# One order of width classes, one form of down product: a mixture-of-experts layer on Trainium2

## The chip, the cores and the metric

The kernel runs on one core of a Trainium2 chip. TensorE (PE) multiplies, with its weight loads shown apart (PEld); VectorE (DVE), ScalarE (ACT) and GpSimd (POOL) work beside it; SyncE (SP) issues the large transfers. The metric is the device time of one launch in microseconds (us), the median over runs. Every trace below is one profiled execution.

## The reference, cut to what matters

A decoder layer over 1024 tokens of 1024 channels: a recurrent branch and an attention branch (their code is untouched), then a mixture of experts. A router picks 4 of 32 experts for every token. For each expert, with its own weights:

```
gu  = x_blk @ w_gate_up[e] + b_gate_up[e]        # 1024 -> 2048
g   = min(gu[:, :1024], 7);  u = clip(gu[:, 1024:], -7, 7)
act = (u + 1) * (g * sigmoid(1.702 * g))
y   = act @ w_down[e] + b_down[e]                # 1024 -> 1024
out[token] += gate * y                           # on top of the residual
```

The 4096 pairs of token and expert are spread unevenly. The reference's routing of its own inputs gives these tokens per expert, sorted: 56, 69, 72, 85, 92, 100, 107, 108, 111, 112, 117, 119, 119, 122, 124, 128, 131, 132, 138, 141, 143, 145, 148, 155, 157, 158, 160, 162, 167, 168, 172, 178. No expert has over 256, so there are 32 items of work, one for each expert.

## The kernel before, in words

Stages A to C compute the two branches and the router. Stage D counts the tokens of each expert on DVE (L1420 to L1503), gives each item a width class from `WIDTHS` (L34) and sorts the items by class, widest first. Stage E works through them. `by_class` (L1657) writes one loop for each class on every engine, with the matmuls cut to `w` columns; items of one class follow one another.

One item `i` of width `w`, by engines:

- SP loads 12.6 MB of weights through six slots of 2 MB (`load`, L1700), each as soon as DVE has consumed it; two orders of the loads, for items up to `n_wide` and behind it (L1742).
- The weights come as 12 chunks: c0 to c7 gate and up, c8 to c11 down. A chunk is split into two half-precision parts: ACT makes the high part (`split_hi`, L1861), DVE the rest (`split_lo`, L1975, with `largest` for a later check). Rings of six (four in narrow items) hold the parts.
- PE makes three half-precision passes over a split chunk (`split_chunk`, L2181). An item with `w >= 128` (`halves`, L1642) does this for all 12 chunks. A narrower item does it for c0 to c7 and multiplies the down chunks in float32 straight from the staged weights (`whole_chunk`, L2196).
- DVE clips gate and up (L2035, L2042) and makes the product (L2052); where down is split too, ACT rounds it (L1920) and DVE takes the rest (`activated_lo`, L2057, signal `a_s`). DVE's order is fixed: clip of chunk c, then split of chunk c+4.
- At an item's end PE turns the next item's gathered rows (`turn_rows`, L2137) in groups of four transposes: two groups of 128 tokens when `w` is at most 128, four otherwise. ACT (L1869) and DVE (L2004) split what came out, cut to the columns that the present width needs; the order by falling width makes that enough for the next item. The third and fourth group come after PE's wait for the last `a_s` (L2239).
- ACT then alternates `y_bias` (L1912, out of PSUM), the next item's `split_hi` for c0 to c3, and the gated rows `y_part` (L1880); it reloads a table (L1929) and splits c4 of the new item. POOL gathers rows (L1783) and adds the results to the output (L1797).

The order of PE around an item's end (L2234 to L2243):

```
down_lo_sy(0); pe.wait_ge(a_s, NP * i + 3)
down(0, 0, 6); down_lo_sy(1); down(1, 0, 6)
pe.wait_ge(a_s, NP * i + 4)
down(0, 6, KT)
for g in range(2, 2 * blocks(w)): turn_rows(i + 1, g, w, ...)
down(1, 6, KT)
for j in range(2, NP): down_lo_sy(j); down(j); turn_y(i, j - 2, w)
```

and of ACT (L1948 to L1967): x_part 0 and 1, next_hi(0), x_part 2 and up, y_bias(0), next_hi(1), y_bias(1), next_hi(2), y_bias(2), y_part(0), next_hi(3), y_bias(3), y_part(1).

Of the kernel before, what the change touches and what calls it, by code (L numbers as in the profile page):

```python
# [21 lines left out]
P = 128  # L22
# [1293 lines left out]
def stage_d(nc, m, a):  # L1316
# [9 lines left out]
    with ExitStack() as ctx:  # L1326
# [87 lines left out]
        def _(dve):  # L1414
# [13 lines left out]
            step(dve.tensor_tensor(kind[:], over[:, 1:NV + 1, :], over[:, 0:NV, :], ALU.subtract))  # L1428
# [62 lines left out]
            for g in range(0, NG, BATCH):  # L1491
# [60 lines left out]
def stage_e(nc, m, a, fast):  # L1552
# [21 lines left out]
    with ExitStack() as ctx:  # L1574
# [82 lines left out]
        def by_class(eng, n_items, early, body):  # L1657
# [12 lines left out]
            with eng.If(early[-1] > 0):  # L1670
                lo = 0
                for v in range(EARLY):
                    one_class(lo, early[v], WIDTHS[v])
                    lo = early[v]
                eng.nop()
            lo = early[-1]
            for v in range(EARLY, NV):
                hi = border(eng, v)
                one_class(lo, hi, WIDTHS[v])
                lo = hi  # L1680
# [18 lines left out]
        def _(sp):  # L1699
# [10 lines left out]
            def run():  # L1710
# [31 lines left out]
                if fast:  # L1742
                    n_wide = sp.value_load(m.n_wide[0:1, 0:1], min_val=0, max_val=ITEMS - 1)
                    with sp.If(n_wide > 0):
                        with sp.Fori(0, n_wide) as i:
                            e_next = expert(sp, i + 1)
                            load_up(i, e_next)
                            load_down(i, e_next)
                            load_later(i)
                        sp.nop()  # L1750
                    with sp.If(n_items - 1 > n_wide):
                        with sp.Fori(n_wide, n_items - 1) as i:
                            e_next = expert(sp, i + 1)
# [106 lines left out]
        def _(act):  # L1860
# [3 lines left out]
            def x_part(i, g, w, first=False):  # L1864

                act.wait_ge(x_mm, NP * i + x_step(w) * (g + 1))
                k0, b = 4 * (g % 2), g // 2
                n = min(w - b * P, P)
                act.activation((x_hi if fast else x_f)[:, k0:k0 + 4, b * P:b * P + n],  # L1869
                               x_bank(g, first)[:].rearrange("p a (b n) -> p (a b) n", n=P)[:, :, 0:n], ACT.Copy, scale=SX  # L1870
                               ).then_inc(x_hi_s, x_step(w))
# [14 lines left out]
            def run():  # L1886
# [3 lines left out]
                for g in range(NP):  # L1890
                    x_part(0, g, CHUNK, True)
# [7 lines left out]
                def body(i, w):  # L1899
# [5 lines left out]
                    def y_bias(j):  # L1905
# [3 lines left out]
                        if fast and not halves(w) and j % 2 == 1:  # L1909
                            act.sem_inc(down_lo_s, 2)  # L1910
                        for h in range(2):
                            ins = act.activation(y_t[:, 2 * j + h, 0:w], p_d[j % 2][:, h, 0:w], ACT.Identity,  # L1912
                                                 bias=bias[:, 16 + 2 * j + h:17 + 2 * j + h],
                                                 scale=1.0 / SW / SA if halves(w) else 1.0 / S2)
# [15 lines left out]
                    for c in range(NG):  # L1930
                        if c % 2 == 1:
                            silu(c // 2)
                        if halves(w):
# [3 lines left out]
                            split_hi(c + RI, ring(c + RI, w))  # L1937
                            if c % 2 == 1:
                                activated_hi(c // 2)
                        else:  # L1940
                            act.wait_ge(gu_mm, NG * i + c + 1)
                            if fast:
                                cc = c + RI
                                act.wait_ge(w_in[slot(cc % NG)], 16 * (i + cc // NG + 1))
                                split_hi(cc % NG, ring(cc, w))
# [14 lines left out]
                    if halves(w):  # L1960
                        next_hi(2)
                    y_bias(2)
                    y_part(i, 0, blocks(w))
                    if halves(w):
# [9 lines left out]
        def _(dve):  # L1974
# [15 lines left out]
            def fold(k, wide):  # L1990
# [3 lines left out]
                dve.wait_ge(down_peak_s, NP * (k + 1) if wide else NP)  # L1994
# [3 lines left out]
            def x_part(i, g, w, first=False):  # L1998
                dve.wait_ge(x_hi_s, NP * i + x_step(w) * (g + 1))
                b = g // 2  # L2000
                n = min(w - b * P, P)
                k0 = 4 * (g % 2)
                r = (slice(None), slice(k0, k0 + 4), slice(b * P, b * P + n))
                dve.scalar_tensor_tensor(out=x_lo[r], in0=x_bank(g, first)[:].rearrange("p a (b n) -> p (a b) n", n=P)[:, :, 0:n],  # L2004
                                         scalar=SX, in1=x_hi[r], op0=ALU.mult, op1=ALU.subtract).then_inc(x_lo_s, x_step(w))
# [4 lines left out]
            def run():  # L2010
                if fast:
# [5 lines left out]
                    for g in range(NP):  # L2017
                        x_part(0, g, CHUNK, True)
# [3 lines left out]
                def body(i, w):  # L2022
# [24 lines left out]
                    def product(j):  # L2047
# [4 lines left out]
                        dve.scalar_tensor_tensor(out=up[j % 2][:, :, 0:w] if halves(w) else a_f[:, 2 * j:2 * j + 2, 0:w],  # L2052
# [319 lines left out]
```

## Time and profile before

| what | value |
|---|---|
| median of 3 runs | 1895.47 us (1894.23 to 1898.2) |
| span of the profiled execution | 1890.9 us, so 4.6 us under the median |
| PE busy | 1792.1 us (95%) |
| DVE busy | 1427.3 us (75%) |
| ACT busy | 1252.4 us (66%) |
| POOL busy | 429.0 us (23%) |
| mean granted clock | 0.978 |
| moved | 479.08 MB |

The span runs from the first to the last instruction. The profiled execution's own time is this span and what lies around it; the 4.6 us are taken for the latter. Stage E begins at 591.5 us. The forms of its matmuls tell the classes: one item each of 184 and 176 columns, three of 168, four of 160, two of 152, three of 144, two of 136, six of 128, five of 112 and five of 96.

### The profile page before, as it was taken

The page shows a single profiled execution, that of the slowest core. Times are in us where ns is not written, and L with a number is a line of the kernel's source. Part 1 is how long each engine was busy: PE and PEld are TensorE (multiplying, and loading weights), DVE is VectorE, ACT ScalarE, POOL GpSimd, SP SyncE. Part 2 cuts the span into 40 slices and gives each one's busy share as a digit, 9 for nine tenths or more (in the row PEclk, how much of TensorE's full clock was granted, in tenths as well). Part 3 has the DMA queues.
Part 4 walks back from the last instruction along what each step waited for, and adds up shares of the span by engine and source line. Part 5 has one row for each costly group of instructions (what it writes and reads, how often), then busy time and mean ns, then how long its engine had stood idle before and what let it go on. Part 6 is the DMA issues. An engine that isn't in the chain of part 4 may idle for free.

```text
span 1890.9 us, 54214 instructions
## 1 busy us (share of the span) xinstructions
PE 1792.1 (95%) x21982; PEld 1645.4 (87%) x21982; DVE 1427.3 (75%) x2714; ACT 1252.4 (66%) x1661; POOL 429.0 (23%) x304
## 2 busy tenths in 40 slices
PE   8999988988987999999999999999999999999996
PEld 7777765667866999999999999998999899999996
DVE  5553647765357888888888889999999977767755
ACT  6565337873114777777777888778887876657654
POOL 4000000001003111111112322323233334434433
PEclk9999999999987999999999999999999999999998
DMA  5211001004539889999999999999999999999993
GB/s 152 56 45 45 23 28 41 1 1 151 175 120 346 287 297 306 307 308 328 321 323 321 335 327 345 324 349 341 352 366 351 359 357 372 373 375 375 367 374 111
DMA packets 251409, 479.08 MB, mean 253 GB/s; under 512 B 17312, under 2 KB 38096, under 8 KB 251264
## 3 DMA queue, kind: packets, MB, share of 16 engines
q1 hardware_dynamic: 231040, 443.59, 64.8%
q0 software_dynamic: 20256, 33.94, 8.2%
q8 instruction: 77, 1.26, 0.3%
q14 instruction: 36, 0.29, 0.0%
HBM read 466.96 MB, written 47.19 MB: 272 GB/s over the span
## 4 chain that ended last, share of the span: by engine, by line
PE 40%; DVE 11%; issue 11%; ACT 6%; DVEq 0%; ACTq 0%; POOLq 0%; POOL 0%
PE E_p_d L2200 6%; DVE E_w_lo L1984 6%; PE E_p_g L2188 4%; PE E_p_g L2190 4%; PE E_p_g L2191 4%; PE E_p_u L2190 4%; PE E_p_u L2188 4%; PE E_p_u L2191 4%; PE E_p_d L2188 3%; PE E_p_d L2191 3%; PE E_p_d L2190 3%; ACT E_w_hi L1862 3%; DVE E_up L2042 2%; PE E_p_t L2146 2%; PE E_p_t L2161 2%
## 5 line engine op out<-in xcount | busy, mean ns | idle before, releaser
L1984 DVE SCALAR_TENSOR_TENSOR E_w_lo<-E_w_st,E_w_hi 128x2048 f16<-128x2048 f32 x348 | 794.8, 2284 | 28.8 <-ACT E_w_hi L1862 27.4
L1862 ACT ACTIVATE E_w_hi<-E_w_st 128x2048 f16<-128x2048 f32 x348 | 661.4, 1906 | 25.4 <-PEq L1326 24.2
L2188 PE MATMUL E_p_g<-E_x_hi,E_w_hi 128*128 128x128 f16 (+9 forms) x2048 | 368.7, 223 | 4.2 <-DVE E_w_lo L1984 4.0
L2190 PE MATMUL E_p_g<-E_x_lo,E_w_hi 128*128 128x128 f16 (+9 forms) x2048 | 368.6, 223 | 1.5 <-issue 1.5
L2188 PE MATMUL E_p_u<-E_x_hi,E_w_hi 128*128 128x128 f16 (+9 forms) x2048 | 366.9, 222 | 2.1 <-DVE E_w_lo L1984 2.1
L2191 PE MATMUL E_p_g<-E_x_hi,E_w_lo 128*128 128x128 f16 (+9 forms) x2048 | 368.6, 223 | 0.0
L2190 PE MATMUL E_p_u<-E_x_lo,E_w_hi 128*128 128x128 f16 (+9 forms) x2048 | 366.8, 222 | 0.0
L2191 PE MATMUL E_p_u<-E_x_hi,E_w_lo 128*128 128x128 f16 (+9 forms) x2048 | 366.8, 222 | 0.0
L2188 PE MATMUL E_p_d<-E_a_hi,E_w_hi 128*128 128x128 f16 (+7 forms) x1408 | 280.1, 230 | 21.8 <-DVE E_a_lo L2059 17.9
L2190 PE MATMUL E_p_d<-E_a_lo,E_w_hi 128*128 128x128 f16 (+7 forms) x1408 | 280.1, 230 | 0.0
L2191 PE MATMUL E_p_d<-E_a_hi,E_w_lo 128*128 128x128 f16 (+7 forms) x1408 | 280.0, 230 | 0.0
L1797 POOL DMA_INDIRECT out<-E_y_rows,E_idx_out x66 | 153.0, 2317 | 485.1 <-ACT E_y_rows L1880 464.1
L2188 PEld LDWEIGHTS E_p_g<-E_x_hi,E_w_hi 128*128 128x128 f16 x2048 | 201.1, 98 | 6.1 <-DVE E_w_lo L1984 4.9
L2188 PEld LDWEIGHTS E_p_u<-E_x_hi,E_w_hi 128*128 128x128 f16 x2048 | 200.4, 98 | 2.8 <-DVE E_w_lo L1984 2.8
L2191 PEld LDWEIGHTS E_p_g<-E_x_hi,E_w_lo 128*128 128x128 f16 x2048 | 201.1, 98 | 1.8 <-issue 1.7
L2190 PEld LDWEIGHTS E_p_g<-E_x_lo,E_w_hi 128*128 128x128 f16 x2048 | 201.1, 98 | 0.7
L2190 PEld LDWEIGHTS E_p_u<-E_x_lo,E_w_hi 128*128 128x128 f16 x2048 | 200.4, 98 | 0.4
L2191 PEld LDWEIGHTS E_p_u<-E_x_hi,E_w_lo 128*128 128x128 f16 x2048 | 200.4, 98 | 0.0
L2188 PEld LDWEIGHTS E_p_d<-E_a_hi,E_w_hi 128*128 128x128 f16 x1408 | 139.0, 99 | 27.7 <-DVE E_a_lo L2059 17.8
L2200 PE MATMUL E_p_d<-E_a_f,E_w_st 128*128 128x112 f32 (+1 forms) x1280 | 150.2, 276 | 6.5 <-DVE E_a_f L2052 6.4
L2200 PEld LDWEIGHTS E_p_d<-E_a_f,E_w_st 128*128 128x128 f32 x1280 | 146.0, 192 | 10.1 <-issue 6.1
L2190 PEld LDWEIGHTS E_p_d<-E_a_lo,E_w_hi 128*128 128x128 f16 x1408 | 139.1, 99 | 0.7
(408 smaller groups left out, 3293.3 us busy)
## 6 DMA issues: line engine op xcount, KB each, us to landing
E_w_st<-in_w_gate_up SPq DMA_DIRECT2D x130, 2048.0 KB, 10.8
E_w_st<-in_w_down SPq DMA_DIRECT2D x64, 2048.0 KB, 10.8
A_w_st<-in_w_in SPq DMA_DIRECT2D x20, 512.0 KB, 3.9
A_x_rows<-in_x SPq DMA_DIRECT2D x8, 512.0 KB, 8.0
C_x_res<-in_x SPq DMA_DIRECT2D x8, 512.0 KB, 4.6
x_rows<-C_x SPq DMA_DIRECT2D x8, 512.0 KB, 5.1
out<-C_x SPq DMA_DIRECT2D x8, 512.0 KB, 5.9
h_rows<-C_h SPq DMA_DIRECT2D x8, 512.0 KB, 4.4
```

Of the source, the lines that this page charges most:

```text
L1797: pool.indirect_dma_start(a.out[0], bass.IndirectOffsetOnAxis(ap=idx_out[:, b:b + 1], axis=0), y_rows[:, b, :], None, bounds_check=token_m ...
L1862: act.activation(w_hi[r][:], staged(c), ACT.Copy, scale=SW).then_inc(hi_s if c < NG else down_hi_s, 1)
L1984: dve.scalar_tensor_tensor(out=w_lo[r][:], in0=staged(c), scalar=SW, in1=w_hi[r][:], op0=ALU.mult, op1=ALU.subtract, accum_out=total[:, c: ...
L2042: ins = dve.tensor_scalar(up[j % 2][:, h, 0:w], p_u[j % 2][:, h, 0:w], bias[:, 8 + 2 * j + h:9 + 2 * j + h], S1 * (LIMIT + 1.0), ALU.add, ...
L2146: ins = pe.transpose(bank[:, q // 2, (q % 2) * P:(q % 2 + 1) * P], rows[:, g // 2, k * P:(k + 1) * P], m.ident[:])
L2161: ins = pe.transpose(p_t[j % 2][:, b, h * P:(h + 1) * P], y_t[:, 2 * j + h, b * P:(b + 1) * P], m.ident[:])
L2188: pe.matmul(o_, wh, hi[:, k, 0:w], start=h == 0 and k == 0, stop=False, skip_group_check=True)
L2190: pe.matmul(o_, wh, lo[:, k, 0:w], start=False, stop=False, skip_group_check=True)
L2191: ins = pe.matmul(o_, wl, hi[:, k, 0:w], start=False, stop=k == KT - 1, skip_group_check=True)
L2200: ins = pe.matmul(banks[:, h, 0:w], staged(c)[:, k, h * P:(h + 1) * P], x[:, k, 0:w], start=h == 0 and k == 0, stop=k == KT - 1, skip_grou ...
```

## The change

The class list gets finer at its narrow end (120, 104, 88 and 72 are new) and the items are ordered so that a class of the wide half and one of the narrow half follow each other: 256, 192, then 184, 128, 176, 120, 168, 112, 160, 104, 152, 96, 144, 88, 136, 72. With the counts above the order of items is 184, 3 x 128, 176, 3 x 120, 3 x 168, 4 x 112, 4 x 160, 104, 2 x 152, 96, 3 x 144, 88, 2 x 136, 3 x 72. Every item splits all 12 chunks and makes its down products in three half-precision passes; the float32 form is left to the fallback. Every item turns all four groups of the next item's rows, 128 columns each, since the next item may be wider. SP has one order of loads. `n_wide` and its instruction go; stage D's class difference is written in two instructions.

```
-WIDTHS = (256, 192, 184, 176, 168, 160, 152, 144, 136, 128, 112, 96)
+WIDTHS = (256, 192, 184, 176, 168, 160, 152, 144, 136, 128, 120, 112, 104, 96, 88, 72)
-HALVES = 128
+FIRST = 2
+PAIRS = (NV - FIRST) // 2
+ORDER = WIDTHS[:FIRST] + tuple(WIDTHS[FIRST + PAIRS * side + v] for v in range(PAIRS) for side in range(2))
...
-            step(dve.tensor_tensor(kind[:], over[:, 1:NV + 1, :], over[:, 0:NV, :], ALU.subtract))
+            step(dve.tensor_tensor(kind[:, 0:FIRST, :], over[:, 1:FIRST + 1, :], over[:, 0:FIRST, :], ALU.subtract))
+            step(dve.tensor_tensor(kind[:, FIRST:NV, :].rearrange("p (v a) e -> p a v e", a=2), ...
...
-        def halves(w):
-            return fast and w >= HALVES
-        def ring(c, w):
-            return c % RING if halves(w) else c % RI
+        def ring(c):
+            return c % RING
...
-                    one_class(lo, early[v], WIDTHS[v])
+                    one_class(lo, early[v], ORDER[v])
...
-                    n_wide = sp.value_load(m.n_wide[0:1, 0:1], min_val=0, max_val=ITEMS - 1)
...
+                    with sp.Fori(0, n_items - 1) as i:
+                        e_next = expert(sp, i + 1)
+                        load_up(i, e_next)
+                        load_down(i, e_next)
+                        load_later(i)
...
-                n = min(w - b * P, P)
-                act.activation((x_hi if fast else x_f)[:, k0:k0 + 4, b * P:b * P + n],
+                act.activation((x_hi if fast else x_f)[:, k0:k0 + 4, b * P:(b + 1) * P],
...
-                    for g in range(2, 2 * blocks(w)):
-                        x_part(i + 1, g, w)
+                    for g in range(2, 2 * NB):
+                        x_part(i + 1, g)
                     y_bias(0)
-                    if halves(w):
+                    if fast:
                         act.wait_ge(gu_mm, NG * i + NG)
                         next_hi(1)
...
-                    if halves(w):
-                        x_part(i + 1, 0, w)
-                        x_part(i + 1, 1, w)
+                        x_part(i + 1, 0)
+                        x_part(i + 1, 1)
                         split_lo(NG * (i + 1) + 1, 0, 0, True)
-                        for g in range(2, 2 * blocks(w)):
-                            x_part(i + 1, g, w)
+                        for g in range(2, 2 * NB):
+                            x_part(i + 1, g)
                         for c in range(1, RI):
                             split_lo(NG * (i + 1) + c + 1, c, c, True)
...
                     def down(j, k0=0, k1=KT):
-                        if halves(w):
+                        if fast:
                             split_chunk(NG + j, p_d[j % 2], a_hi, a_lo, k0, k1)
...
-                    for g in range(2, 2 * blocks(w)):
-                        turn_rows(i + 1, g, w, lambda: pe.wait_ge(x_out_s, NP * (i + 1) + g - 1))
+                    for g in range(2, 2 * NB):
+                        turn_rows(i + 1, g, lambda: pe.wait_ge(x_out_s, NP * (i + 1) + g - 1))
```

## Rows read from the trace of the kernel before

**Rows 1.** The page, parts 1 and 2: busy time; GB/s in 40 slices.

```profile
PE 1792.1 (95%) x21982; PEld 1645.4 (87%) x21982; DVE 1427.3 (75%) x2714; ACT 1252.4 (66%) x1661; POOL 429.0 (23%) x304
GB/s 152 56 45 45 23 28 41 1 1 151 175 120 346 287 297 306 307 308 328 321 323 321 335 327 345 324 349 341 352 366 351 359 357 372 373 375 375 367 374 111
```

**Rows 2.** Windows over stage E: items of 184 to 136; 128 to 96; the last.

```profile
core 0: us, PE busy (x) PEld busy (x) DVE busy (x) ACT busy (x) POOL busy (x), PEclk, DMA share, GB/s
591.50:1292.00 700.50, 692.38 (x9729) 685.05 (x9729) 615.39 (x1108) 534.86 (x671) 167.41 (x114) 0.99 0.94 322
1292.00:1840.10 548.10, 525.32 (x8365) 518.12 (x8365) 449.85 (x863) 395.48 (x498) 200.31 (x105) 0.99 1.03 364
1840.10:1890.90 50.80, 34.93 (x544) 33.85 (x541) 28.42 (x66) 23.40 (x33) 17.46 (x9) 0.89 0.40 130
```

**Rows 3.** Windows of one item each: 168, 160, 136, 128, 128, 112, 96 columns.

```profile
739.10:784.70 45.60, 45.40 (x610) 45.17 (x608) 39.06 (x70) 33.77 (x43) 8.79 (x7) 1.00 0.90 305
917.70:961.40 43.70, 43.50 (x610) 43.26 (x609) 38.39 (x70) 33.58 (x43) 8.45 (x7) 1.00 0.92 316
1210.40:1250.30 39.90, 38.35 (x610) 37.59 (x610) 37.16 (x69) 32.43 (x43) 12.28 (x7) 1.00 0.99 344
1329.10:1366.90 37.80, 34.83 (x599) 34.27 (x597) 36.48 (x68) 31.61 (x39) 12.46 (x7) 1.00 1.01 359
1404.70:1443.90 39.20, 36.37 (x598) 35.70 (x597) 37.52 (x70) 32.62 (x39) 12.45 (x7) 0.96 1.01 358
1591.60:1627.50 35.90, 35.86 (x535) 35.54 (x534) 25.66 (x51) 23.12 (x30) 14.07 (x7) 1.00 1.05 374
1734.60:1769.80 35.20, 33.63 (x535) 33.01 (x533) 25.12 (x51) 22.47 (x30) 14.26 (x7) 1.00 1.04 373
```

**Rows 4.** Waits within the 160-column item: who waited, for whom, us, times, longest.

```profile
DVE E_gate L2035 <- PE E_p_g L2191: 1.3, 1, 1.3
PE E_p_d L2188 <- ACT E_y_t L1912: 0.2, 1, 0.2
```

**Rows 5.** Timeline of DVE, end of a 128-column item (start, us, engine, line).

```profile
1358.90 0.42 DVE L2059 SCALAR_TENSOR_TENSOR E_a_lo<-E_up,E_a_hi 128x256 f16<-128x256 f32 x1
1359.68 1.29 DVE L2004 SCALAR_TENSOR_TENSOR E_x_lo<-E_p_t,E_x_hi 128x512 f16<-128x512 f32 x2 [0.20 <-DVE E_peak_min L1996]
1371.97 2.29 DVE L1984 SCALAR_TENSOR_TENSOR E_w_lo<-E_w_st,E_w_hi 128x2048 f16<-128x2048 f32 x1 [0.84 <-ACT E_w_hi L1862]
```

**Rows 6.** Timeline of ACT, end of the same item.

```profile
1360.32 0.63 ACT L1912 ACTIVATE E_y_t<-E_p_d,E_bias 128x128 f32<-128x128 f32 x2 [0.40 <-PE E_p_d L2191]
```

**Rows 7.** Timeline of DVE, end of a 136-column item.

```profile
1240.07 0.43 DVE L2059 SCALAR_TENSOR_TENSOR E_a_lo<-E_up,E_a_hi 128x272 f16<-128x272 f32 x1
```

**Rows 8.** Timeline of ACT, end of the same 136-column item.

```profile
1242.84 0.20 ACT L1869 ACTIVATE E_x_hi<-E_p_t 128x32 f16<-128x32 f32 x1 [0.40 <-PE E_p_t L2146]
1242.93 0.63 ACT L1912 ACTIVATE E_y_t<-E_p_d,E_bias 128x136 f32<-128x136 f32 x2
```

**Rows 9.** Groups by line and form: count, busy us, mean ns, idle before.

```profile
L1869 ACT ACTIVATE E_x_hi<-E_p_t 128x512 f16<-128x512 f32 x44 | 23.5, 584 | 0.0
L2004 DVE SCALAR_TENSOR_TENSOR E_x_lo<-E_p_t,E_x_hi 128x512 f16<-128x512 f32 x44 | 28.4, 686 | 3.3 <-DVE E_peak_min L1996 1.2
L2035 DVE TENSOR_SCALAR E_gate<-E_p_g,E_bias 128x128 f32<-128x128 f32 x48 | 14.5, 344 | 1.8 <-PE E_p_g L2191 1.3
L2035 DVE TENSOR_SCALAR E_gate<-E_p_g,E_bias 128x112 f32<-128x112 f32 x40 | 11.3, 325 | 5.4 <-PE E_p_g L2191 5.2
L1912 ACT ACTIVATE E_y_t<-E_p_d,E_bias 128x128 f32<-128x128 f32 x48 | 15.2, 377 | 3.2 <-PE E_p_d L2191 3.0
L1912 ACT ACTIVATE E_y_t<-E_p_d,E_bias 128x112 f32<-128x112 f32 x40 | 12.0, 351 | 38.4 <-PE E_p_d L2200 38.4
```

**Rows 10.** Window inside the second 128-column item of Rows 3.

```profile
1436.30:1439.70 3.40, 3.32 (x34) 3.09 (x32) 3.40 (x6) 3.40 (x6) 0.00 (x0) 0.50 1.05 382
```

**Rows 11.** Timeline of DVE in stage D: first and last of nine class instructions.

```profile
551.57 0.59 DVE L1426 TENSOR_TENSOR D_over<-D_rem,limit 128x416 f32<-128x416 f32 x1
557.73 0.80 DVE L1445 TENSOR_REDUCE D_jump<-D_start 128x32 f32<-128x384 f32 x1
```

More of the change, by code:

```diff
@@ L1427, in _ @@
                                    m.limit[:].unsqueeze(2).to_broadcast([P, NV + 1, E_]), ALU.is_gt))
-            step(dve.tensor_tensor(kind[:], over[:, 1:NV + 1, :], over[:, 0:NV, :], ALU.subtract))
+            step(dve.tensor_tensor(kind[:, 0:FIRST, :], over[:, 1:FIRST + 1, :], over[:, 0:FIRST, :], ALU.subtract))
+            step(dve.tensor_tensor(kind[:, FIRST:NV, :].rearrange("p (v a) e -> p a v e", a=2),
+                                   over[:, FIRST + 1:NV + 1, :].rearrange("p (a v) e -> p a v e", a=2),
+                                   over[:, FIRST:NV, :].rearrange("p (a v) e -> p a v e", a=2), ALU.subtract))
             step(dve.tensor_copy(share[:], kind[:]))
@@ L1862, in split_hi, with x_part @@
                 act.activation(w_hi[r][:], staged(c), ACT.Copy, scale=SW).then_inc(hi_s if c < NG else down_hi_s, 1)
-            def x_part(i, g, w, first=False):
-                act.wait_ge(x_mm, NP * i + x_step(w) * (g + 1))
+            def x_part(i, g, first=False):
+                act.wait_ge(x_mm, NP * i + g + 1)
                 k0, b = 4 * (g % 2), g // 2
-                n = min(w - b * P, P)
-                act.activation((x_hi if fast else x_f)[:, k0:k0 + 4, b * P:b * P + n],
-                               x_bank(g, first)[:].rearrange("p a (b n) -> p (a b) n", n=P)[:, :, 0:n], ACT.Copy, scale=SX
-                               ).then_inc(x_hi_s, x_step(w))
+                act.activation((x_hi if fast else x_f)[:, k0:k0 + 4, b * P:(b + 1) * P],
+                               x_bank(g, first)[:].rearrange("p a (b n) -> p (a b) n", n=P), ACT.Copy, scale=SX
+                               ).then_inc(x_hi_s, 1)
             def y_part(i, j, nb):
@@ L1908, in y_bias @@
                         act.wait_ge(d_mm, NP * i + j + 1)
-                        if fast and not halves(w) and j % 2 == 1:
-                            act.sem_inc(down_lo_s, 2)
                         for h in range(2):
@@ L1941, in body @@
                             act.wait_ge(gu_mm, NG * i + c + 1)
[L1942 to L1945, printed above, removed]
                         if c < 2:
@@ L1959, in body @@
                     y_bias(1)
-                    if halves(w):
+                    if fast:
                         next_hi(2)
@@ L1963, in body @@
                     y_part(i, 0, blocks(w))
-                    if halves(w):
+                    if fast:
                         next_hi(3)
@@ L1988, in split_lo, with fold, x_part @@
                     largest()
-            def fold(k, wide):
+            def fold(k):
                 dve.wait_ge(fold_s, 2 * k)
                 dve.wait_ge(peak_s, NG * k)
-                dve.wait_ge(down_peak_s, NP * (k + 1) if wide else NP)
+                dve.wait_ge(down_peak_s, NP * (k + 1))
                 dve.tensor_tensor(total_all[:], total_all[:], total[:], ALU.add).then_inc(fold_s, 1)
                 dve.tensor_tensor(peak_min[:], peak_min[:], peak[:], ALU.min).then_inc(fold_s, 1)
-            def x_part(i, g, w, first=False):
-                dve.wait_ge(x_hi_s, NP * i + x_step(w) * (g + 1))
+            def x_part(i, g, first=False):
+                dve.wait_ge(x_hi_s, NP * i + g + 1)
                 b = g // 2
-                n = min(w - b * P, P)
                 k0 = 4 * (g % 2)
-                r = (slice(None), slice(k0, k0 + 4), slice(b * P, b * P + n))
-                dve.scalar_tensor_tensor(out=x_lo[r], in0=x_bank(g, first)[:].rearrange("p a (b n) -> p (a b) n", n=P)[:, :, 0:n],
-                                         scalar=SX, in1=x_hi[r], op0=ALU.mult, op1=ALU.subtract).then_inc(x_lo_s, x_step(w))
+                r = (slice(None), slice(k0, k0 + 4), slice(b * P, (b + 1) * P))
+                dve.scalar_tensor_tensor(out=x_lo[r], in0=x_bank(g, first)[:].rearrange("p a (b n) -> p (a b) n", n=P),
+                                         scalar=SX, in1=x_hi[r], op0=ALU.mult, op1=ALU.subtract).then_inc(x_lo_s, 1)
             n_items = count(dve)
@@ L2136, in _, with turn_rows @@
         def _(pe):
-            def turn_rows(i, g, w, free=None):
+            def turn_rows(i, g, free=None):
                 if g == 0:
@@ L2167, in run @@
             def run():
-                turn_rows(0, 0, CHUNK)
-                turn_rows(0, 1, CHUNK)
+                turn_rows(0, 0)
+                turn_rows(0, 1)
                 n_items = count(pe)
                 early = early_borders(pe)
-                turn_rows(0, 2, CHUNK)
-                turn_rows(0, 3, CHUNK)
+                turn_rows(0, 2)
+                turn_rows(0, 3)
                 if fast:
@@ L2299, in build @@
     m.n_redo = at("n_redo", [1, 1], I32, o + 5 * KIB + 64)
-    m.n_wide = at("n_wide", [1, 1], I32, o + 5 * KIB + 128)
     place = [112 * KIB]
```

67 lines of the change are left out of this document (20 added, 47 removed).

## The prediction, made before the change was run

> **What bounds the kernel now.** I read the page's engine totals first. PE is busy for 95% of the span, which invites the reading that fewer PE columns mean less time; the slices of GB/s say that the load changes along the way, with 287 to 327 in slices 14 to 18 and 366 to 375 near the end [rows 1]. So I split stage E into windows [rows 2] and then looked at single items [rows 3].
>
> The single items show three limits. At 168 and 160 columns PE is busy for all but 0.2 us; 8 columns cost (45.40 - 43.50) = 1.9 us of PE, 0.24 us a column; DVE idles for 43.7 - 38.39 = 5.3 us. At 136 and 128 columns PE idles (38.35 of 39.9, 34.83 of 37.8), and so does DVE a little; 136 columns should cost PE about 37.9 us by the slope (43.7 - 24 x 0.24), the item takes 39.9. Below that, where down is multiplied in float32, PE is full again at 112 (35.86 of 35.9) and nearly so at 96 (33.63 of 35.2), while DVE has 10 us to spare.
>
> What holds the 128-column item is a loop over two engines. Follow DVE: after the last `a_lo` of the item it does the fold, the row parts and four splits; then the split of c4 waits 0.84 us for ACT's high part [rows 5]. ACT's tail is a strict series behind its first `y_bias`, and that begins 1360.32 - 1358.90 = 1.42 us after the start of the last `a_lo` [rows 5, 6]. From the split of c4 on DVE works without a pause up to the next `a_lo`. The loop is therefore: DVE's middle of the item, then ACT's tail.
>
> **The change, part by part.**
>
> *Down in three passes in the ten items of 112 and 96 columns.* It adds four splits to DVE (2.29 us each [rows 5]), four to ACT, and the rounding of `act`. That is over 9 us on a DVE with 10 us to spare, so these items join the loop just described. What they save on PE comes to nothing, because PE is not the last to be ready any more.
>
> *All rows turned in full.* PE turns groups 2 and 3 only after the last `a_lo`, and only when DVE has emptied the bank of the group before (two more waits of PE's queue, with the rest of down and the whole next item behind them). ACT's `y_bias(0)` stands behind the two row parts that come of it. The 136-column item shows this form already: ACT's last row part begins 1242.84 - 1240.07 = 2.77 us after the start of `a_lo`, and `y_bias` 0.09 us behind it, the part being 32 elements long [rows 7, 8]. In full length it takes 0.584 us [rows 9]; less the overlap of 0.11 us (0.20 - 0.09) that is 0.47 us. So `y_bias(0)` starts 2.77 + 0.47 = 3.24 us after `a_lo` in every item, instead of 1.42 us at 128 columns: 1.8 us later, and everything behind it in ACT's series as much. The loop at 128 columns becomes 37.8 + 1.8 = 39.6 us. From below, were ACT out of it, DVE alone would need 37.8 - 0.84 + 1.2 = 38.2 us (two row parts of 0.6 us, [rows 5]); the first is nearer, since the wait of 0.84 us shows that ACT is the later one already.
>
> *Narrower classes.* 112 fewer columns in all (4320 to 4208) save PE 27 us, off the path. In the loop a step from 128 to 112 columns shortens a clip by 344 - 325 = 19 ns and a `y_bias` by 26 ns [rows 9]. The loop holds 14 clips (0.27 us), eight operations over twice the elements (estimated at twice the step, 0.30) and eight `y_bias` (0.21): 0.78 us for 16 columns, 0.39 for 8. That gives 39.6 at 128, 39.2 at 120, 38.8 at 112, 38.4 at 104, 38.0 at 96, 37.7 at 88 and 36.9 at 72. With 3, 3, 4, 1, 1, 1 and 3 items: 118.8 + 117.6 + 155.2 + 38.4 + 38.0 + 37.7 + 110.7 = 616.4 us. The same sixteen experts take 548.1 us now [rows 2] for fifteen, and 35.2 for the last one as its kind does [rows 3]: 583.3. **Plus 33.1 us.**
>
> *The order.* An item of one kind after the other would gain if the 5.3 us that DVE idles in a 160-column item could be used for a narrow one. I see no way: DVE clips chunk c before it splits c+4, so in a wide item it waits for PE at each chunk [rows 4], and PE waits for the last `a_lo` of every item. At the six changes from wide to narrow a small debit remains (the wide item's `y_part` has two pieces in ACT's tail, about 0.7 us, less some lead of PE): 2 us, between -9 and +4.
>
> *Wide items.* PE sets their time. PE waits 0.2 us for `y_bias(0)` at 160 columns [rows 4], so what stands ahead of it now counts: the full row part is about 0.3 us longer than a cut one (a 32-element one takes 0.20 us, the full one 0.584). Eleven items of 152 to 184 columns: 3.3 us. The five of 144 and 136 lie in the loop already; 39.9 + 0.4 at 136 is about what they take with their one disturbance. Nothing.
>
> *The last item.* The next item's splits of c0 to c3 now come behind the last `a_lo` and ahead of the judging and the last rows, where the narrow body had them earlier. Between 0 and 9.2 us (four splits); I take 4, since PE's last transposes run beside them.
>
> *Stage D.* Nine instructions over 384 or 416 elements (4.8 us together, first and last in [rows 11]) grow by a third, at most 1.6 us with the second class difference; the dropped `n_wide` was off the path. 1.5 us.
>
> *Transfers.* 12.6 MB of weights in 38 us are 331 GB/s, under the 373 of the 96-column item [rows 3]: free, and SP's single order follows DVE's own. If loads became late, a slot would cost a few us an item.
>
> *PE's clock.* In the second 128-column item of [rows 3] one stretch of 3.4 us at 0.50 (the 1.2 GHz level), just after PE had waited for `a_lo`, goes with 39.2 - 37.8 = 1.4 us [rows 10]. PE will wait longer there: idle per item goes from 3 us at 128 columns to 14 or so at 72 (38.35 - 64 x 0.24 = 23 busy of 36.9). None to all of sixteen items at 1.4 us: 0 to 22. I take 10, since at 112 and below PE has slack against ACT that hides a part.
>
> A rule of the Trainium skill speaks against the change here: "TensorE: Matmul & The Clock Gate", section "HAM oscillation — how this bites in real kernels", says that a loop whose bursts of matmuls are parted by waits is throttled in each round and pays each time. The trace agrees in some rounds only: [rows 3] has two items of the same width, one with the drop and one without. By the rule the term would be 22 us in place of 10, and the whole 1961.
>
> **Sum.** 33.1 + 2 + 3.3 + 4 + 1.5 + 10 = 53.9 us on a span of 1890.9 us: 1944.8, and with the 4.6 us that the median of the runs lies above it, **1949 us, 2.8% slower**. Its own range, from half the clock term and 8 us on the loop: 1930 to 1968.
>
> **The rivals.**
>
> *DVE's idle time does pay (the other side).* If lead could be carried from a wide item into the narrow one, DVE would never wait. Its work in stage E is 615.4 + 449.9 + 28.4 = 1093.7 us [rows 2], plus ten items with four splits and four `a_lo` (105), row parts (25), less narrower forms (5): 1219 us, and about 15 of tail, against 1299.4 now. That is 64 us faster, 1831 us. It decides from the point where DVE no longer waits at L2035 in wide items. For it speaks that the idle time is there [rows 3]; against it DVE's order and the wait for `a_lo`. 5%.
>
> *Half clock in every narrow item.* The waits ahead of `a_lo` grow to several us and each narrow item pays 1.4 us or twice that: 22 to 45 us in place of 10, 1961 to 1984, say 1972. For it: [rows 10]. Against it: PE's work after the drop is short in narrow items, and only part of it is in the loop. The skill's rule quoted above would make this the likeliest case; two like items of which one shows a drop keep it below the forecast. 20%.
>
> *ACT's tail does not bind, DVE alone does.* Then 1.4 us less for each of sixteen items: 1927, and 1917 without the clock term. For it: the 0.84 us are a small margin. Against it: the 136-column item already runs longer than either PE or DVE needs. 15%.
>
> *No difference.* Savings on PE (27 us of columns, and at 96 columns whatever part of the 1.6 us of idle PE is due to transfers) would have to reach the end and cancel the loop. 4%.
>
> **How the numbers follow.** The forecast has 56%, the rivals 5, 20, 15 and 4. A measurement of this kernel tells about 0.2% from no change, 3.8 us. Faster: 0.05; same: 0.04; slower: 0.91. The range takes in DVE alone (1917) and the dear end of the clock rival (1984); what it leaves out is the first rival, the fourth and some 6% at the ends.
>
> **What would show it.** In the profile after, narrow items of 37 to 40 us that shorten by 0.4 us for 8 columns; DVE over 95% busy in them and PE at 60 to 90%; DVE's split of c4 still waiting for ACT; ACT's last row part beginning about 2.8 us after the start of `a_lo`; wide items within 0.5 us of now; more stretches at 0.50. The prediction is wrong if narrow items fall below 36 us, if a wide item following narrow ones is more than 3 us shorter than its class is now, or if splits wait for weights.

## The result: 2.6% slower, and the profile after

The changed kernel takes 1945.3 us (median of 4 runs, 1941.62 to 1945.93) against 1894.85 us for the kernel before beside it (4 runs, 1894.2 to 1898.2): ratio 1.0263, 95% interval [1.0248, 1.0277]. The profiled execution has a span of 1944.2 us at a mean granted clock of 0.966. The forecast was 1949 us, a span of 1944.8. The total is nearly exact; its terms are not, as the section on the prediction shows.

From the page of the kernel after: span, busy time, GB/s in 40 slices, and two groups of instructions (busy us, mean ns | idle before, releaser).

```profile
span 1944.2 us, 56138 instructions
PE 1755.9 (90%) x22750; PEld 1594.8 (82%) x22750; DVE 1562.9 (80%) x2906; ACT 1360.3 (70%) x1773; POOL 420.2 (22%) x303
GB/s 148 54 44 44 22 55 12 1 37 151 163 179 329 292 362 325 301 335 351 340 309 300 306 352 349 353 321 301 299 355 323 337 362 311 346 342 340 341 327 47
L1963 DVE SCALAR_TENSOR_TENSOR E_w_lo<-E_w_st,E_w_hi 128x2048 f16<-128x2048 f32 x388 | 885.8, 2283 | 25.4 <-ACT E_w_hi L1848 25.4
L2157 PE MATMUL E_p_d<-E_a_hi,E_w_hi 128*128 128x112 f16 (+13 forms) x2048 | 377.5, 227 | 90.6 <-DVE E_a_lo L2037 72.2
```

Against [rows 1], DVE has 135.6 us more work and PE 36.2 us less, and the kernel is 53.3 us longer: the work moved onto engines that were late. The 25 us in which the split (now L1963) waits for ACT's high part, and the 72 us in which PE waits for `a_lo`, are two ends of one loop.

Windows of the kernel after: the seven stretches of narrow items (3 x 128, 3 x 120, 4 x 112, 104, 96, 88, 2 x 72 columns), then the last item, also of 72. Columns as in [rows 2].

```profile
651.30:770.90 119.60, 109.95 (x1814) 106.96 (x1813) 112.42 (x206) 98.24 (x121) 37.70 (x21) 0.99 0.99 345
818.80:937.10 118.30, 105.69 (x1814) 103.01 (x1812) 111.31 (x205) 97.25 (x121) 37.05 (x21) 0.97 1.00 348
1075.00:1230.50 155.50, 134.40 (x2418) 130.50 (x2416) 147.84 (x274) 128.91 (x161) 48.98 (x28) 0.97 1.00 350
1406.80:1444.70 37.90, 32.42 (x607) 31.13 (x605) 35.85 (x67) 31.38 (x41) 11.41 (x7) 0.95 1.02 353
1529.10:1566.50 37.40, 29.05 (x606) 27.66 (x606) 35.51 (x68) 31.00 (x41) 11.14 (x7) 1.00 1.03 354
1690.30:1728.30 38.00, 30.11 (x605) 28.64 (x604) 35.54 (x68) 31.28 (x42) 11.22 (x7) 0.91 1.02 353
1810.10:1884.90 74.80, 52.69 (x1210) 49.77 (x1210) 69.82 (x136) 61.58 (x80) 22.11 (x13) 0.91 0.99 350
1884.90:1944.20 59.30, 27.68 (x616) 25.48 (x614) 43.94 (x92) 34.81 (x47) 17.73 (x11) 0.81 0.27 83
```

Fifteen narrow items take 581.5 us, 33.4 more than in [rows 2]. PE's share falls from 92% to 70% as the items narrow; DVE stays at 93 to 95%. The last item takes 59.3 us (50.8 before). What is left for the sixteen wide items, 1884.9 - 597.1 - 581.5 = 706.3 us, is 5.8 more, and stage E starts at 597.1 instead of 591.5. The four together: 33.4 + 8.5 + 5.8 + 5.6 = 53.3 us, the whole difference.

Single items of the kernel after: 128 columns without and with a stretch of lower clock, 112 columns with and without one, 160 columns.

```profile
690.50:730.10 39.60, 36.07 (x606) 35.15 (x604) 37.82 (x70) 32.69 (x41) 12.55 (x8) 1.00 1.00 353
730.10:770.90 40.80, 37.70 (x606) 36.57 (x604) 38.41 (x71) 33.27 (x41) 13.14 (x8) 0.96 0.96 336
1112.90:1152.00 39.10, 33.95 (x606) 33.02 (x605) 37.36 (x70) 32.45 (x41) 12.49 (x8) 0.96 1.01 357
1152.00:1191.10 39.10, 32.41 (x607) 31.48 (x605) 37.37 (x70) 32.45 (x41) 12.49 (x8) 1.00 0.98 347
1274.60:1318.70 44.10, 43.53 (x611) 43.29 (x609) 39.25 (x70) 34.14 (x43) 8.82 (x7) 1.00 0.92 315
```

The end of the 128-column item without a drop, DVE first, then ACT (start, us, engine, line):

```profile
720.30 0.41 DVE L2037 SCALAR_TENSOR_TENSOR E_a_lo<-E_up,E_a_hi 128x256 f16<-128x256 f32 x1
735.19 2.29 DVE L1963 SCALAR_TENSOR_TENSOR E_w_lo<-E_w_st,E_w_hi 128x2048 f16<-128x2048 f32 x1 [0.84 <-ACT E_w_hi L1848]
...
722.45 1.20 ACT L1854 ACTIVATE E_x_hi<-E_p_t 128x512 f16<-128x512 f32 x2 [1.13 <-PE E_p_t L2115]
723.54 0.62 ACT L1895 ACTIVATE E_y_t<-E_p_d,E_bias 128x128 f32<-128x128 f32 x2
```

These answer to [rows 5 to 8]: `a_lo` at 720.30, ACT idle until PE has turned the third group, its two late row parts, and `y_bias(0)` at 723.54, 3.24 us after `a_lo`. At the other end DVE stands 0.84 us ahead of the split of c4, waiting for ACT. From `y_bias(0)` to that split it is 735.19 - 723.54 = 11.65 us, and in the kernel before 1371.97 - 1360.32 = 11.65 us too [rows 5, 6]: ACT's series is as long as it was and starts later.

### The profile page after: what moved, and what is told of

The parts are those of the page before. It is cut to its first block, busy times and chain, and to the rows that moved or that the text cites. A ratio compares the mean times of both kernels' runs of the same rounds, so it can differ in the third digit from the quotient of the medians.

```text
span 1944.2 us, 56138 instructions
## 1 busy us (share of the span) xinstructions
PE 1755.9 (90%) x22750; PEld 1594.8 (82%) x22750; DVE 1562.9 (80%) x2906; ACT 1360.3 (70%) x1773; POOL 420.2 (22%) x303
## 4 chain that ended last, share of the span: by engine, by line
PE 27%; DVE 16%; issue 15%; ACT 10%; ACTq 1%; DVEq 0%; POOLq 0%; POOL 0%
DVE E_w_lo L1963 9%; ACT E_w_hi L1848 5%; PE E_p_d L2157 3%; PE E_p_d L2160 3%; PE E_p_d L2159 3%; PE E_p_g L2157 3%; PE E_p_g L2159 3%; PE E_p_g L2160 3%; PE E_p_u L2157 3%; PE E_p_u L2160 3%; PE E_p_u L2159 3%; ACT E_y_t L1895 3%; PE E_p_t L2115 2%; DVE E_up L2020 2%; DVE E_gate L2013 2%
## 5 line engine op out<-in xcount | busy, mean ns | idle before, releaser
L1963 DVE SCALAR_TENSOR_TENSOR E_w_lo<-E_w_st,E_w_hi 128x2048 f16<-128x2048 f32 x388 | 885.8, 2283 | 25.4 <-ACT E_w_hi L1848 25.4
L2157 PE MATMUL E_p_d<-E_a_hi,E_w_hi 128*128 128x112 f16 (+13 forms) x2048 | 377.5, 227 | 90.6 <-DVE E_a_lo L2037 72.2
L2159 PE MATMUL E_p_d<-E_a_lo,E_w_hi 128*128 128x112 f16 (+13 forms) x2048 | 377.3, 227 | 0.0
L2160 PE MATMUL E_p_d<-E_a_hi,E_w_lo 128*128 128x112 f16 (+13 forms) x2048 | 377.2, 227 | 0.0
L2157 PE MATMUL E_p_g<-E_x_hi,E_w_hi 128*128 128x112 f16 (+13 forms) x2048 | 360.0, 222 | 15.5 <-issue 8.0
L2157 PE MATMUL E_p_u<-E_x_hi,E_w_hi 128*128 128x112 f16 (+13 forms) x2048 | 358.5, 221 | 7.8 <-DVE E_w_lo L1963 7.8
L2160 PE MATMUL E_p_g<-E_x_hi,E_w_lo 128*128 128x112 f16 (+13 forms) x2048 | 359.9, 222 | 1.5 <-issue 1.5
L2159 PE MATMUL E_p_g<-E_x_lo,E_w_hi 128*128 128x112 f16 (+13 forms) x2048 | 359.8, 222 | 1.5 <-issue 1.5
L2159 PE MATMUL E_p_u<-E_x_lo,E_w_hi 128*128 128x112 f16 (+13 forms) x2048 | 358.4, 221 | 0.1
L2160 PE MATMUL E_p_u<-E_x_hi,E_w_lo 128*128 128x112 f16 (+13 forms) x2048 | 358.4, 221 | 0.0
L2160 PEld LDWEIGHTS E_p_d<-E_a_hi,E_w_lo 128*128 128x128 f16 x2048 | 208.3, 102 | 0.0
```

Source lines behind the costliest of these rows:

```text
L1963: dve.scalar_tensor_tensor(out=w_lo[r][:], in0=staged(c), scalar=SW, in1=w_hi[r][:], op0=ALU.mult, op1=ALU.subtract, accum_out=total[:, c: ...
L2157: pe.matmul(o_, wh, hi[:, k, 0:w], start=h == 0 and k == 0, stop=False, skip_group_check=True)
L2159: pe.matmul(o_, wh, lo[:, k, 0:w], start=False, stop=False, skip_group_check=True)
L2160: ins = pe.matmul(o_, wl, hi[:, k, 0:w], start=False, stop=k == KT - 1, skip_group_check=True)
```

## The experiments

**1. The narrow items' down products alone.** The kernel before, falling order and cut rows kept.

```
-HALVES = 128
+HALVES = 96
```

> Kernel before with one edit: all items split their down chunks too; old classes, falling order, rows turned only as far as needed. Theory (the loop of DVE's middle and ACT's tail sets narrow items, and turning the rows in full lengthens it by 1.8 us): the ten items of 112 and 96 columns go from 35.8 and 35.2 us to about 37.0 and 36.4 us, the last item ends some 5 us later, so about 1912 us (+17). Rival (the three-pass down products are the whole cost): 1940 us or more. Items of 128 columns stay at 37.8 us.

Measured: 1912.85 us, ratio 1.0102 [1.0077, 1.0128]. The profiled execution took 1905.75 us, the shortest of the four (the others 1912.27 to 1914.2), so its items show where time goes, and the medians how much. Items of 128, 112 and 96 columns and the last:

```profile
1363.80:1401.60 37.80, 34.83 (x599) 34.26 (x597) 36.48 (x68) 31.61 (x39) 12.47 (x7) 1.00 1.02 359
1589.00:1626.20 37.20, 31.16 (x599) 30.57 (x598) 35.87 (x68) 31.26 (x39) 13.89 (x7) 1.00 1.02 364
1736.60:1773.10 36.50, 29.38 (x599) 28.41 (x597) 35.17 (x68) 30.79 (x39) 13.86 (x7) 0.95 1.03 364
1846.80:1904.00 57.20, 30.84 (x608) 29.12 (x605) 42.76 (x87) 33.58 (x43) 17.06 (x9) 0.83 0.31 99
```

PE drops from 35.86 to 31.16 us at 112 columns and the item is 1.3 us longer [rows 3]: PE, which filled this item, is relieved, but DVE goes from 25.66 to 35.87 us and stands in the loop, which is now the longer. The last item pays 6.4 us.

**2. The full turning, with old classes and falling order.** The changed kernel with the old class list, and with stage D's class difference back in one instruction. It is one step from experiment 1, apart from the dropped `n_wide`: with `HALVES` at 96, `n_wide` takes in all items, so SP's loads come in one order there already.

```
-WIDTHS = (256, 192, 184, 176, 168, 160, 152, 144, 136, 128, 120, 112, 104, 96, 88, 72)
+WIDTHS = (256, 192, 184, 176, 168, 160, 152, 144, 136, 128, 112, 96)
-ORDER = WIDTHS[:FIRST] + tuple(...)
+ORDER = WIDTHS
```

> Changed kernel with the old twelve classes in falling order: against the run before it adds only the turning of all rows. Theory: 16 narrow items 1.8 us longer (128 columns 39.6 us, 112 near 39.0), 3 us in the wide items, a few us of slower clock: 1945 to 1950 us. Rival (DVE alone binds, ACT's tail does not): 0.4 us an item, about 1920 us.

Measured: 1946.72 us, ratio 1.0277 [1.0245, 1.0309]. Items of 128 (two), 112 and 96 columns:

```profile
1420.40:1459.70 39.30, 36.10 (x606) 35.17 (x605) 37.53 (x70) 32.37 (x41) 12.25 (x8) 1.00 0.98 345
1459.70:1500.30 40.60, 37.43 (x607) 36.78 (x606) 37.92 (x70) 32.76 (x41) 10.91 (x8) 0.96 0.94 333
1618.20:1657.20 39.00, 33.93 (x606) 33.02 (x604) 37.27 (x70) 32.34 (x41) 12.40 (x8) 0.96 0.98 345
1773.20:1811.70 38.50, 30.49 (x606) 29.17 (x605) 36.85 (x70) 32.09 (x41) 12.38 (x8) 0.96 0.98 345
```

At full clock the 128-column item is 1.5 us longer than in experiment 1 (39.3 for 37.8), and those of 112 and 96 columns are 1.8 and 2.0 longer. The other five of 128 columns, each with a stretch of lower clock, take 40.3 to 40.7 us, 2.5 to 2.7 more than in experiment 1, so part of what the full turning costs goes with the clock. It is the larger part of the loss: 34 us between the medians.

**3. The order alone.** The changed kernel with all its classes, in falling order (stage D's class difference in one instruction).

```
-ORDER = WIDTHS[:FIRST] + tuple(...)
+ORDER = WIDTHS
```

> Changed kernel with its sixteen classes in falling order: only the alternation is undone. Theory (no lead is carried from a wide item to a narrow one, the order costs about 2 us): 1943 us, within 4 us of the changed kernel's 1945. Rival (DVE's idle time in wide items pays for narrow ones): falling order is slower by tens of us, 1970 or more. Second rival (each change of class costs): 1935 or less.

Measured: 1947.85 us, ratio 1.029 [1.0261, 1.0319]. Items of 160 and 112 columns, and the fifteen narrow items in one window:

```profile
877.40:921.50 44.10, 43.53 (x611) 43.30 (x609) 39.24 (x70) 34.12 (x43) 8.82 (x7) 1.00 0.92 315
1614.90:1654.00 39.10, 34.03 (x607) 33.11 (x606) 37.38 (x70) 32.45 (x41) 12.51 (x8) 0.96 0.98 346
1297.90:1884.50 586.60, 498.43 (x9060) 481.52 (x9061) 556.33 (x1034) 483.66 (x601) 181.87 (x104) 0.95 0.98 344
```

The single items have the lengths of the alternating kernel's items of those widths, with the same busy times. The fifteen narrow items take 586.6 us, 5.1 more than the 581.5 in alternation. Part of that is the clock, which drops in other items here (two of the three of 128 columns, for one there). From the start of stage E to the end of the span falling order is 3.6 us longer (1350.7 us for 1347.1), and the 4.6 us by which stage E starts earlier in this execution (592.5 for 597.1) hide that in the span. So alternation gains a few us at most, not clear of noise in the medians, and not the tens of the rival that carries DVE's idle time from wide items into narrow ones; that rival falls. Nor do the finer classes show against experiment 2.

**4. ACT's order.** The changed kernel with ACT's two late row parts behind `y_bias(0)` and the high part of c1. DVE and PE keep their orders.

```
-                    for g in range(2, 2 * NB):
-                        x_part(i + 1, g)
                     y_bias(0)
                     if fast:
                         act.wait_ge(gu_mm, NG * i + NG)
                         next_hi(1)
+                    for g in range(2, 2 * NB):
+                        x_part(i + 1, g)
                     y_bias(1)
```

> Changed kernel with one edit on ACT: the row parts 2 and 3 come behind next_hi(1) instead of ahead of y_bias(0). The same work in another order. Theory (ACT's tail behind the late row parts is in the loop): y_bias(0) begins about 1.4 us after the start of the last a_lo instead of 3.2, about 0.8 us less in each of 21 items of 144 columns and fewer, and 0.4 us in each wide item, where PE waits for y_bias(0): about 1923 us. Rival (DVE alone binds): narrow items keep their 39 us, only the wide ones gain: 1940 us.

Measured: 1917.67 us, ratio 1.0127 [1.0102, 1.0152]: 28 of the 34 us of experiment 2 come back. Items of 112 and 160 columns; the last `a_lo` and `y_bias(0)` of that of 112, and DVE's split of c4 in the item after it:

```profile
1097.60:1135.70 38.10, 33.68 (x607) 32.92 (x605) 37.17 (x70) 32.27 (x41) 12.20 (x8) 0.96 1.01 363
1255.70:1299.00 43.30, 43.30 (x610) 43.24 (x608) 39.09 (x69) 33.96 (x43) 9.15 (x7) 1.00 0.94 320
...
1127.39 0.38 DVE L2037 SCALAR_TENSOR_TENSOR E_a_lo<-E_up,E_a_hi 128x224 f16<-128x224 f32 x1
1128.69 0.60 ACT L1895 ACTIVATE E_y_t<-E_p_d,E_bias 128x112 f32<-128x112 f32 x2 [0.31 <-PE E_p_d L2160]
1141.21 2.29 DVE L1963 SCALAR_TENSOR_TENSOR E_w_lo<-E_w_st,E_w_hi 128x2048 f16<-128x2048 f32 x1 [0.52 <-ACT E_w_hi L1848]
```

With the work of every engine unchanged, only the place of two activations was moved, and `y_bias(0)` begins 1128.69 - 1127.39 = 1.30 us after `a_lo`. So the queue behind ACT's wait for PE's late transposes is shown to cost the changed kernel 28 us. Not all of these belong to the change: some 12 come back in the sixteen wide items of the profiled execution (43.3 us for 44.1 at 160 columns, where the kernel before took 43.7), and experiment 8 finds 7.5 us of the same kind in the kernel before. In the wide item PE is now busy all the time: the wait for `y_bias(0)` is gone there too.

**5. A second step on ACT's tail.** Experiment 4, and the activation that reloads the table moved behind the high part of c4.

```
-                    act.wait_ge(warm_s, i + 1)
-                    act.activation(warm[:], warm[:], ACT.Silu).then_inc(warm_s, 1)
                     for c in range(NG):
...
+                        if c == 0:
+                            act.wait_ge(warm_s, i + 1)
+                            act.activation(warm[:], warm[:], ACT.Silu).then_inc(warm_s, 1)
```

> The run with ACT's new order plus one more move: the small activation that makes ACT reload its table (1.28 us) goes behind the split of c4 instead of ahead of it. Theory (a rest of ACT's tail is still in the loop: 0.52 us of wait ahead of the split of c4 at 112 columns): the wait goes, 0.5 us in each of 16 narrow and 5 middle items, about 1908 us; DVE then waits for nothing and the loop is DVE alone. Rival (what is left is DVE's own work, or the reload only moves the wait to the split of c5): 1918 us.

Measured: 1939.14 us, ratio 1.0236 [1.0218, 1.0254]. A miss by 31 us. Groups of ACT, the table loads of stage E: first those of experiment 4, then of this run; then ACT and DVE at an item's start in this run:

```profile
L1912 ACT ACT_TABLE_LOAD x32 | 41.1, 1283 | 2.4 <-issue 1.9
...
L1848 ACT ACT_TABLE_LOAD x32 | 41.1, 1283 | 2.5 <-issue 2.0
L1925 ACT ACT_TABLE_LOAD x32 | 41.1, 1283 | 0.6
...
1146.29 1.28 ACT L1848 ACT_TABLE_LOAD   x1
1147.58 1.91 ACT L1848 ACTIVATE E_w_hi<-E_w_st 128x2048 f16<-128x2048 f32 x1
1149.51 1.28 ACT L1925 ACT_TABLE_LOAD   x1
...
1149.52 2.29 DVE L1964 SCALAR_TENSOR_TENSOR E_w_lo<-E_w_st,E_w_hi 128x2048 f16<-128x2048 f32 x1 [0.42 <-ACT E_w_hi L1848]
1153.84 2.29 DVE L1964 SCALAR_TENSOR_TENSOR E_w_lo<-E_w_st,E_w_hi 128x2048 f16<-128x2048 f32 x1 [1.03 <-ACT E_w_hi L1848]
```

With the Silu activation no longer first, a load still stands ahead of ACT's high part of c4, and a second one behind it, in each of the 32 items. DVE's split of c4 still waits 0.42 us, and that of c5 now 1.03 us: the edit lengthened the tail that it was to shorten. It still speaks for the theory: 1.28 us more on ACT make the second 112-column item about 1.0 us longer (39.15 us in place of 38.12 from its first matmul to the next item's), and the item of 160 columns, where PE is full, not at all (43.3 both). The Trainium skill ("ScalarE activation tables: per-element evaluation and per-set limits", section "Table sets in the compiler and the runtime") says that loads are placed block by block, by the longest run that one set serves. The rows show two loads in a round, one ahead of the high part (a Copy) and one ahead of Silu; whether that rule makes them, no run here shows, since none shows which functions one set serves.

**6. PE's clock.** The changed kernel with 10 to 16 matmuls that nobody reads (512 columns each), in PE's two waits for `a_lo`, in items of up to 128 columns.

```
+                    def fill(n):
...
+                            for _ in range(n):
+                                pe.matmul(p_g[0][:]..., m.ident_b[:], ..., start=True, stop=True)
...
+                    fill(4 if w >= 128 else 6 if w >= 120 else 10)     # ahead of the wait for NP * i + 3
...
+                    fill(6)                                            # ahead of the wait for NP * i + 4
```

> Changed kernel with matmuls of no use (512 columns each, 4 to 10 of them) put into PE's two waits for a_lo in items of 128 columns and fewer. Theory (the stretches at 1.2 GHz cost what the prediction set, 10 us): they go from the narrow items and the time falls to about 1935 us. Reading of single items of the changed kernel (a drop costs about 1.1 us at 128 columns, nothing at 112, 0.6 at 72): about 1940 us. Rival (half clock costs every narrow item 1.4 us): 1923 us. If filling delays PE: 1945 or more.

Measured: 1942.19 us, ratio 1.0247 [1.0226, 1.0269]. Windows of the third item of 128, the second of 112, the one of 88 and the first two of 72 columns:

```profile
729.90:769.90 40.00, 38.28 (x617) 36.06 (x615) 38.23 (x70) 33.07 (x41) 12.95 (x8) 1.00 0.97 342
1111.20:1150.20 39.00, 35.78 (x622) 32.82 (x620) 37.27 (x70) 32.35 (x41) 12.41 (x8) 1.00 1.01 357
1688.60:1725.80 37.20, 30.91 (x622) 27.16 (x622) 35.20 (x68) 30.93 (x42) 10.89 (x7) 1.00 1.03 350
1808.70:1844.60 35.90, 27.24 (x620) 23.45 (x621) 33.72 (x67) 29.87 (x40) 9.85 (x6) 1.00 1.02 350
1844.60:1882.30 37.70, 27.36 (x624) 23.54 (x623) 36.14 (x73) 31.68 (x42) 12.30 (x8) 1.00 0.99 353
```

Their clock is 1.00 throughout, as in all fifteen narrow items. The 128-column item gains 40.8 - 40.0 = 0.8 us, that of 88 columns 38.0 - 37.2 = 0.8, the two of 72 together 74.8 - 73.6 = 1.2, that of 112 nothing. The whole is 3.1 us between medians and 3.6 between spans, with overlapping intervals, so the medians alone show no gain. Item by item the fifteen narrow ones take 577.7 us in place of 581.5, 3.8 less; the last gains 0.9, and an item of 136 columns loses 1.2 to a stretch of lower clock of its own.

**7. and 8. The kernel before with a better ACT order.** First the order of experiment 4 together with the moved table reload (the latter in items whose down is split).

```
+                    if not halves(w):
+                        warm_up()
...
+                        if c == 0 and halves(w):
+                            warm_up()
```

> Kernel before with ACT's tail changed alone (row parts 2 and 3 behind next_hi(1), the table reload behind the split of c4, both only in items of 128 columns and more). Theory (ACT's tail is in the loop of the items of 128 to 144 columns already, and PE waits for y_bias(0) in wide ones): 0.8 us in six items of 128, 1.5 us in two of 136, 0.3 in three of 144, 0.36 in eleven wide ones: about 1882 us, faster than both kernels. Rival (DVE alone binds those items): 1891 us, the wide items' share only.

Measured: 1899.45 us, ratio 1.0019 [1.0008, 1.0029]; a miss by 17 us, with 22 second loads in the items whose down is split, the cause found in experiment 5. Then the order alone, which is the edit of experiment 4 made in the kernel before:

```
-                    for g in range(2, 2 * blocks(w)):
-                        x_part(i + 1, g, w)
                     y_bias(0)
                     if halves(w):
                         act.wait_ge(gu_mm, NG * i + NG)
                         next_hi(1)
+                    for g in range(2, 2 * blocks(w)):
+                        x_part(i + 1, g, w)
                     y_bias(1)
```

> The kernel before with one edit: ScalarE computes y_bias(0) and the parts behind it ahead of the later row parts of the next item's x_hi, not behind them. The warm activation stays where it was. My theory: in an item whose down product is split, VectorE waits at its end for ScalarE, so the edit takes that wait away there. The wide items lost 0.36 us each when the same order was tried together with another edit, so 11 of them give 4 us; the two items of 136 lose 1.0 to 1.3 us each, the three of 144 some 0.3; the items of 128 columns and fewer are not split, VectorE there has slack, and nothing changes. Sum about 7 us: 1888 us, ratio 0.996. Rival: ScalarE's order matters only where every row is turned, as in the changed kernel; then the time is that of before within 0.2%, 1891 to 1899.

Measured: 1886.98 us (9 runs) against 1894.52 (14 runs), ratio 0.9962 [0.9945, 0.9979]: 7.5 us faster than the kernel before, a small difference, but its interval leaves out 1. Items of 168, 160, 136 and 128 columns:

```profile
740.20:785.40 45.20, 45.20 (x610) 45.14 (x608) 38.82 (x70) 33.62 (x43) 10.72 (x7) 1.00 0.91 308
917.40:960.70 43.30, 43.30 (x611) 43.23 (x609) 38.25 (x70) 33.41 (x43) 10.31 (x7) 1.00 0.94 319
1206.80:1246.00 39.20, 38.19 (x609) 37.55 (x609) 36.74 (x70) 32.75 (x43) 13.91 (x7) 1.00 1.01 348
1399.30:1437.10 37.80, 34.85 (x598) 34.28 (x597) 36.48 (x68) 31.62 (x39) 12.45 (x7) 1.00 1.01 358
```

Against [rows 3]: 0.4 us less at 168 and 160 columns, where PE now waits for nothing, 0.7 at 136, nothing at 128, whose rows have no late parts.

With the better order in both kernels the changed one is still some 30 us slower: 1917.67 us (experiment 4) against 1886.98, with the kernel before at 1894.7 and 1894.5 beside them. Of the change's 50 us the place of the two activations thus explains about 20. The down products alone cost 18 (experiment 1); if the parts add up, a dozen is left, which was not taken apart.

## Why the prediction was right, and which of its terms were not

**The loop at 128 columns: right, and shown.** `y_bias(0)` was put at 3.24 us after `a_lo` and begins 3.24 us after it; the item was put at 39.6 us and takes 39.6 without a drop of the clock (the second of the three; the first, behind a wide item, takes 39.1, and the third 40.0 in experiment 6). Experiment 4 moves nothing but these activations and gets 28 us back. The rival in which DVE alone binds was priced at 1927 us, 1917 without the clock term. It fell, since ACT's tail does bind in the changed kernel; experiment 4, which shortens that tail, ends at 1917.67, with 0.52 us of the wait left. DVE, put at over 95% busy in narrow items, is at 93 to 95%.

**The loop below 128: the slope was mis-sized.** I took 0.39 us for 8 columns. Without drops 128 columns take 39.6 us and 72 take 37.7 (the second of experiment 6), 1.9 us over seven steps: about 0.3 each. That narrowest item is 0.8 us dearer than the 36.9 forecast; DVE's busy time falls by only 37.82 - 36.14 = 1.7 us from the one to the other. The first 72-column item, behind a wide one, takes 35.9.

**Order: put at +2, and the traces point the other way.** The first narrow item behind a wide one is about 1.1 us shorter than its like (38.0 against 39.1 at 112 columns), but the first of that class in falling order is short too (38.4). The narrow items behind it show no lead, and the next wide item either none (44.1 us at 160 columns in either order) or a debit (41.8 for 40.7 at the first of 144). In all, alternation is some 4 us shorter in stage E (experiment 3), part of it the clock, and the medians do not tell the two apart; that lies inside the stated -9 to +4.

**PE's clock: the term was too large.** Put at 10 us; the fifteen narrow items gain 3.8 without the drops (experiment 6), and the rival with 22 to 45 us falls. Stretches at the lower level are many, as feared: ten of the fifteen hold one or two. Five of the ten pay 0.6 to 0.8 us (one of 128 and one of 120 columns, that of 88, both of 72), five nothing: at 112 columns an item with one takes the same 39.1 us as one without. That PE's slack hides them, as the prediction had it, is not the whole of it, since PE has more slack at 88 and 72 columns than at 112; those three items have two stretches each (clock 0.91). What decides it was not looked into. So "TensorE: Matmul & The Clock Gate" of the Trainium skill (section "HAM oscillation — how this bites in real kernels") is borne out in that throttled rounds are frequent behind waits, and not in that each pays.

For the fifteen narrow items the forecast was 579.5 - 548.1 = 31.4 us of loop, 10 of clock and 2 of order, 43.4 together; measured 33.4, of which 29.6 stay without the drops. Three other terms were too small and make up for it:

- **Wide items: 5.8 us for 3.3.** The wait of PE for `y_bias(0)` grew as said, from 0.2 [rows 4] to 0.6 us, in the 160-column item of the kernel after:

```profile
DVE E_gate L2013 <- PE E_p_g L2160: 1.3, 1, 1.3
PE E_p_d L2157 <- ACT E_y_t L1895: 0.6, 1, 0.6
```

  That is 0.4 us an item (44.1 for 43.7 at 160 columns), and the eleven come to 3.4 as forecast. The items of 144 and 136 columns, which I had left at nothing, pay the rest, 2.4 us: those of 144 take 41.8, 41.0 and 41.1 us in place of 40.3, 40.6 and 40.8.
- **The last item: 8.5 us for 5.7** (1.7 as a narrow item and 4 for its end). Experiment 1 already shows 6.4 without wide rows or the new order: the four splits behind the last `a_lo` come with the split down product, and in the kernel after they fill the time from 1916.6 to 1928.0 us, ahead of the judging.
- **The start of stage E: 5.6 us for 1.5.** The class instructions grew as estimated, from 6.96 us between the start of the first and the end of the last [rows 11] to 8.42, now:

```profile
554.11 0.72 DVE L1428 TENSOR_TENSOR D_over<-D_rem,limit 128x544 f32<-128x544 f32 x1
561.51 1.02 DVE L1450 TENSOR_REDUCE D_jump<-D_start 128x32 f32<-128x512 f32 x1
```

  The rest of the 5.6 is not the change's as far as the runs tell: with stage D as it was, stage E starts at 591.5 us in the kernel before and at about 595.5 in experiment 8; with it changed, at 592.6 in experiment 4 and 597.1 here. What sets this scatter was not looked into; the four terms of the 53.3 us carry it, one execution each.

So the sign and the size of the main term were understood ahead. That the total came within 4 us is partly luck: -10.0 in the narrow items and +2.5, +2.8 and +4.1 elsewhere cancel to -0.6. The rest of the miss is the step from span to median, put at 4.6 us and 1.1 here (1945.3 - 1944.2). The 4.6 were taken for what lies around the span; in the other executions of the kernel before that is 2.2 to 3.3 us.

Three slips in the working changed nothing: slices 14 to 18 of the GB/s run from 287 to 308, not to 327; the nine class instructions take 5.4 us, not 4.8; and the sum of the first rival leaves 65 us, not 64.

## What to carry to other kernels

Before an engine is relieved, look at which engine each item waits for last: here PE was the busiest. At 128 columns it had nothing to give, and at 112, where it did set the time, what relieved it put DVE and ACT in its place. When one engine's queue alternates between consumers, put what waits for the latest producer behind what others wait for; two activations in another order were worth 28 us in one kernel and 7.5 in the other. Make such a repair in both kernels before a change is judged by it: here the change still loses some 30 us. And the sum over terms should be kept by stage, so that errors that cancel are seen.

## What the runs showed of the hardware

A stretch at 1.2 GHz (a granted clock of 0.50) behind a wait did not cost the same everywhere: 0.8 us in a 128-column item (experiment 6), nothing in one of 112. With the Silu activation first in the loop body stage E had 32 table loads (experiment 4); moved behind the high part of c4 it had 64 (experiment 5), each of 1283 ns. In both runs the next activation began 1.29 us after the start of a load (1146.29 to 1147.58).
